# First v stage in a hand-computed list order, TensorE transposes for nine tiles, and other buffers and orders in an eight-core Trainium2 trunk kernel

## What is computed

```python
def trunk_layer(x, pool_buf, conv_buf, start_pos, pre_g, w_in, v_g, w_s, b_s,
                w_pg, pool_scale, conv_w, w_out, post_g):
    h = rmsnorm(x, pre_g)                                   # 1024 wide
    proj = jnp.einsum('bld,de->ble', h, w_in)
    u, v, z_a, p, z_b, xc, bg, cg, z_c = jnp.split(proj, IN_SPLITS, axis=-1)
    a_out, vn = chunk_gmlp(u, v, v_g, w_s, b_s)             # vn = rmsnorm(v, v_g), 768 wide
    b_out, new_pool = pool_mixer(p, pool_buf, start_pos, w_pg, pool_scale)
    c_out, new_conv = short_conv(xc, bg, cg, conv_buf, conv_w)
    mix = jnp.concatenate([a_out * jax.nn.silu(z_a), b_out * jax.nn.silu(z_b),
                           c_out * jax.nn.silu(z_c)], axis=-1)
    out = jnp.einsum('ble,ed->bld', mix, w_out)
    return x + rmsnorm(out, post_g), new_pool, new_conv, vn
```

## Time and profile before

| what | value |
| --- | --- |
| median of the runs shown | 2111.47 us |
| span of the profiled execution, slowest core (core 1) | 2096.3 us |
| spans of the eight cores | 2079.0 to 2096.3 us |
| TensorE busy | 2009.7 us, 96% of the span |
| VectorE, ScalarE, GpSimd busy | 52%, 27%, 17% |
| v stage of layer 0, first matmul to last | 25.75 to 82.8 us |
| bytes moved by DMA | 190.64 MB, mean 91 GB/s |

### The profile page before, as it was taken

How to read it: one execution, slowest core, us unless ns; L and a number is a source line. 1 busy time by engine, 2 the same in 40 slices (tenths; PEclk the granted TensorE clock), 3 DMA queues, 4 the chain that set the end, 5 groups by cost and what they waited for, 6 DMA issues and landing times.

```text
span 2096.3 us, 32513 instructions; the slowest of 8 cores (2079.0 to 2096.3 us)
## 1 busy us (share of the span) xinstructions
PE 2009.7 (96%) x10792; PEld 985.7 (47%) x10792; DVE 1086.2 (52%) x1592; ACT 574.4 (27%) x1117; POOL 366.2 (17%) x698
## 2 busy tenths in 40 slices
PE   4899999999989999999998999999999899999998
PEld 2445544444444544444454455444445345444443
DVE  3665555545455555554545555554554655555433
ACT  3431122222333122222332312222323221222211
POOL 4400010033320001103331001011333100110011
PEclk9999999999999999999999999999999999999999
DMA  9832333386333224418624323553861432234143
GB/s 233 159 55 39 66 62 60 61 180 182 96 70 58 37 61 81 79 35 200 193 52 75 63 31 67 70 81 65 205 174 35 80 66 40 43 61 70 68 153 131
DMA packets 141812, 190.64 MB, mean 91 GB/s; under 512 B 80976, under 2 KB 86736, under 8 KB 141648
## 3 DMA queue, kind: packets, MB, share of 16 engines
q0 software_dynamic: 41040, 71.39, 22.7%
q1 hardware_dynamic: 100608, 117.16, 19.5%
HBM read 199.70 MB, written 42.35 MB: 115 GB/s over the span
## 4 chain that ended last, share of the span: by engine, by line
PE 74%; DVE 7%; POOL 6%; DMA 5%; issue 5%; ACT 2%; SPq 1%; DVEq 0%; ACTq 0%; POOLq 0%
PE ps L389 59%; PE ps L672 7%; PE ps L435 6%; POOL sb_stats L382 5%; DVE sb_ar L368 3%; DVE sb_ar L364 3%; DMA sb_samp<-sp_in 2%; DMA sb_hT<-sb_hbuf 1%; POOL sb_stats L380 1%; ACT sb_hbuf L360 1%; DMA vs_o<-sb_ar 1%; PE ps L580 1%; PE ps L550 1%; ACT sb_ar L360 1%; SPq L373 0%
## 5 line engine op out<-in xcount | busy, mean ns | idle before, releaser
L389 PE MATMUL ps<-sb_hT,sb_ring 128*128 128x512 bf16 (+1 forms) x7040 | 1337.5, 349 | 0.3
L389 PEld LDWEIGHTS ps<-sb_hT,sb_ring 128*128 128x128 bf16 x7040 | 630.9, 98 | 653.7 <-issue 19.9
L360 ACT ACTIVATE sb_ar<-ps 128x512 f32<-128x512 f32 (+3 forms) x576 | 355.9, 622 | 852.3 <-PE ps L389 543.0
L672 PE MATMUL ps<-sb_wout,sb_mix 128*128 128x512 bf16 x2176 | 470.3, 379 | 3.0 <-issue 3.0
L672 PEld LDWEIGHTS ps<-sb_wout,sb_mix 128*128 128x128 bf16 x2176 | 212.6, 98 | 259.4 <-issue 3.6
L316 POOL DMA_DIRECT2D sb_ring<-w_t x176 | 94.8, 543 | 1018.5 <-PE ps L389 574.7
L435 PE MATMUL ps<-sb_ring,sb_hT 128*128 128x512 bf16 x1088 | 190.8, 340 | 46.6 <-DMA sb_hT<-sb_hbuf 33.1
L364 DVE TENSOR_TENSOR sb_ar<-ps,sb_ar 128x512 f32<-128x512 f32 (+1 forms) x240 | 145.7, 607 | 157.9 <-PE ps L389 155.8
L368 DVE SCALAR_TENSOR_TENSOR sb_ar<-sb_pcx,sb_convw,sb_ar 128x512 f32<-128x512 f32 x192 | 144.3, 752 | 92.8 <-ACT sb_ar L645 82.4
L368 DVE SCALAR_TENSOR_TENSOR sb_hbuf<-sb_ar,sb_stats,sb_pre_bc 128x1024 bf16<-128x1024 f32 x68 | 87.4, 1285 | 170.5 <-POOL sb_stats L382 158.1
L364 DVE TENSOR_TENSOR sb_pcx<-ps,sb_ar 128x512 f32<-128x512 f32 x96 | 66.5, 692 | 208.4 <-PE ps L389 208.4
(11 more groups left out here) (45 smaller groups left out, 489.8 us busy)
## 6 DMA issues: line engine op xcount, KB each, us to landing
sb_ring<-w_t POOLq DMA_DIRECT2D x176, 256.0 KB, 4.9
x_mid<-sb_ar SPq DMA_DIRECT2D x51, 512.0 KB, 3.0
...
```

Of the source, the lines that this page charges most:

```text
L360: return emit(ACT, lambda a: a.activation(out=out, in_=in_, func=func, scale=scale, **kw), reads=reads, writes=writes)
L389: ins = pe.matmul(bank(b, n), lhsT=wa.ap[:, k, :], rhs=hT[:, k, c0:c0 + n], start=(k == 0), stop=(k == 7))
L672: ins = pe.matmul(bank(b + half), lhsT=mix[:, k, j * 128:(j + 1) * 128], rhs=wout[:, k, half * 512:(half + 1) * 512], start=(k == 0), stop ...
```

## The change

- Layer 0's v stage is emitted in the order that a new function, `plan_first`, computes: a list scheduler with fixed durations and landing times, whose steps are sq, rs, nm (norm: square, rstd, scale), tp and ev (transpose on TensorE, copy out of PSUM) or dt (DMA transpose), mm (the 16 matmuls), vs, vr, vn (the same for v). Tiles 0 to 8 are transposed on TensorE, 8 transposes into one bank, and copied out by VectorE (even tiles) or ScalarE (odd ones); tiles 9 to 16 go by DMA as before.
- x tiles of layer 0 go into twelve buffers: four in `ar`, eight in the space of `wout`. Tiles 3 to 11 wait in SP's queue for pieces of w_v: tile 3 for piece 1, tile 4 for piece 3, tile 5 for piece 5, tiles 6 to 11 for piece 7.
- `pre_g` and `v_g` of layer 0 come as one row each (`rows0`, 7 KB together) and are spread over the partitions by four f32 matmuls with a row of ones, then copied by VectorE. A dummy activation is issued first on ScalarE.
- PSUM banks of layer 0's v stage are fixed: v tiles use three pairs (0 to 5) in turn, transposes banks 6 and 7.
- `sp_in` is loaded after the norm of tile 6 in layer 0, and in the out stage of the layer before (at tile 3) for layers 1 to 3.
- `b_stage` begins with slot 0 of the scratch ring.
- `c_stage` takes the chunks in the order 4, 0, 1, 2, 3.
- The last tile's norm of a layer follows the next layer's first v tile. There are 16 columns of statistics for 8.

Core of the diff, with the new functions:

```diff
@@ plan_first (new; the loop picks the ready step that can start first)
+    land_x = [5.0, 7.0, 9.0] + [12.5 + 2.2 * j for j in range(NT - 3)]
+    land_w = [9.5 + 1.4 * k for k in range(8)]
+    for j in range(NT):
+        steps["sq", j] = ("ACT", 1.25, [])
+        steps["rs", j] = ("POOL", 1.1, [("sq", j)])
+        steps["nm", j] = ("DVE", 1.28, [("rs", j)])
+        if j < N_PE_T:
+            steps["tp", j] = ("PE", 0.6, [("nm", j)])
+            steps["ev", j] = ("ACT" if j % 2 else "DVE", 1.15, [("tp", j)])
+            steps["mm", j] = ("PE", 2.6, [("ev", j)])
+        else:
+            steps["dt", j] = ("SP", 1.3, [("nm", j)])
+            steps["mm", j] = ("PE", 2.6, [("dt", j)])
+        steps["vs", j] = ("ACT", 1.0, [("mm", j)])
+        steps["vr", j] = ("POOL", 1.1, [("vs", j)])
+        steps["vn", j] = ("DVE", 1.02, [("vr", j)])
...
@@ helpers
+        def load_x0(j, after=()):
+            s = j % XSLOTS
...
+        def pe_transpose(j, b):
+            hb = j % NHB
+            pt = ps[:, 512 * b:512 * b + 512].bitcast(BF16)
+
+            def f(pe):
+                for k in range(8):
+                    ins = pe.transpose(pt[:, k * 128:(k + 1) * 128], hbuf[:, hb, k * 128:(k + 1) * 128], cstb[:, 0, :])
+                return ins
+            emit(PE, f, reads=[R_hb[hb], R["cstb"]], writes=[bank_res[b]])
+
+        def evac_transpose(j, b, q):
+            src = ps[:, 512 * b:512 * b + 512].bitcast(BF16).rearrange("p (k t) -> p k t", k=8)
+            dst = hT[:, :, j * 128:(j + 1) * 128]
...
@@ b_stage, c_stage
+            st["ar"] = 0
...
-                for ci, (c0, n) in enumerate(CHUNKS):
+                for ci in (4, 0, 1, 2, 3):
+                    c0, n = CHUNKS[ci]
...
@@ layer 0
+        emit(DVE, lambda v: v.memset(one, 1.0), writes=[r_one])
+        emit(SP, lambda s_: s_.dma_start(out=g_row, in_=rows0[:, 0:D]), writes=[r_row], dsem=d_row)
+        load_x0(0)
+        load_x0(1)
+        load_x0(2)
+        emit(SP, lambda s_: s_.dma_start(out=v_row, in_=rows0[:, D:D + WA]), writes=[r_vrow], dsem=d_vrow)
...
+        for j in range(3, XSLOTS):
+            load_x0(j, after=[wv0.kres[min(2 * j - 5, 7)].w])
...
+        spread(g_row, r_row, D, pre_bc[:], R["pre"], 0)
+        spread(v_row, r_vrow, WA, vb_bc[:], R["vb"], 2)
+        for kind, j in plan_first():
...
+            elif kind == "nm":
+                norm_h(j, stat_of[j])
+                if j + XSLOTS < NT:
+                    load_x0(j + XSLOTS)
+                if j == 6:
...
+                    sp_dma(samp[:], sp_in[0], [], [R["samp"]], d_c["samp"])
...
+                if j in (5, 7):
+                    ring_try()
+                elif j == 9:
+                    load_wpg(0)
+                elif j == 11:
+                    load_spatial(0)
@@ all layers
-                need(W[l]["v"])
-                for j in range(NT):
+                for j in range(1, NT):
                     v_job(l, j)
...
-            sp_dma(samp[:], sp_in[l], [], [R["samp"]], d_c["samp"])
...
+                if not last and j == 3:
+                    sp_dma(samp[:], sp_in[l + 1], [], [R["samp"]], d_c["samp"])
                 out_ew(l, j, b)
             if not last:
-                norm_h(NT - 1, norm_sq(NT - 1))
-                t_job(NT - 1)
+                need(W[l + 1]["v"])
+                v_job(l + 1, 0)
+                norm(NT - 1)
```

More of the change, by code:

```diff
@@ L62, in host_consts, with plan_first @@
     return cb.reshape(128, 256), np.ascontiguousarray(fac.reshape(128, 64))
+N_PE_T = 9
+XSLOTS = 12
+def plan_first():
+    land_x = [5.0, 7.0, 9.0] + [12.5 + 2.2 * j for j in range(NT - 3)]
+    land_w = [9.5 + 1.4 * k for k in range(8)]
+    free = {"PE": 0.0, "ACT": 0.0, "DVE": 0.0, "POOL": 0.0, "SP": 0.0}
+    done = {}
+    order = []
+    steps = {}
+    for j in range(NT):
[12 more added lines that the diff above has]
+        steps["vn", j] = ("DVE", 1.02, [("vr", j)])
+    lead = {"sq": 0.0, "rs": 0.0, "nm": 0.0, "tp": 0.2, "ev": 0.3, "dt": 0.3, "mm": 1.0,
+            "vs": 1.2, "vr": 1.2, "vn": 1.3}
+    nxt = {"mm": 0, "sq": 0}
+    left = dict(steps)
+    while left:
+        best = None
+        for (kind, j), (eng, dur, before) in left.items():
+            if any(d in left for d in before) or nxt.get(kind, j) != j:
+                continue
+            t = max([free[eng]] + [done[d] + 0.12 for d in before])
+            end = None
+            if kind == "sq":
+                t = max(t, land_x[j])
+                if j >= NHB:
+                    i = j - NHB
+                    gone = ("tp", i) if i < N_PE_T else ("dt", i)
+                    if gone in left:
+                        continue
+                    t = max(t, done[gone] + (0.0 if i < N_PE_T else 2.0))
+            elif kind == "tp" and j >= 2:
+                if ("ev", j - 2) in left:
+                    continue
+                t = max(t, done["ev", j - 2])
+            elif kind == "mm":
+                if j >= 3:
+                    if ("vn", j - 3) in left:
+                        continue
+                    t = max(t, done["vn", j - 3])
+                if j >= N_PE_T:
+                    t = max(t, done["dt", j] + 2.2)
+                end = t
+                for k in range(8):
+                    end = max(end, land_w[k]) + 0.325
+            key = (t, lead[kind] + j)
+            if best is None or key < best[0]:
+                best = (key, kind, j, eng, t, t + dur if end is None else end)
+        _, kind, j, eng, t, end = best
+        free[eng] = done[kind, j] = end
+        del left[kind, j]
+        if kind in nxt:
+            nxt[kind] += 1
+        order.append((kind, j))
+    return order
@@ L242, in build_nc @@
         R_ar = [Res() for _ in range(NAR)]
[L243 removed]
+        R_stat = [Res() for _ in range(NSTAT)]
         R_xd = [Res() for _ in range(NT)]
@@ L692, in out_ew @@
             sp_dma((y_o if l == DEPTH - 1 else x_mid)[j], x, rx, [R_xd[j]], d_xst[j])
-        AHEAD = 4
+        emit(POOL, lambda g: g.memset(neghalf[:], -0.5), writes=[R["neghalf"]])
+        emit(ACT, lambda a_: a_.activation(out=stats[:, 0:1], in_=neghalf[:], func=AF.Square),
+             reads=[R["neghalf"]], writes=[R_stat[0]])
+        g_row = mix[0:1, 0, :].bitcast(F32)[:, 0:D]
+        v_row = mix[0:1, 1, :].bitcast(F32)[:, 0:WA]
+        one = mix[0:1, 2, :].bitcast(F32)[:, 0:128]
+        r_row, r_vrow, r_one = Res(), Res(), Res()
@@ new lines, in spread @@
+        def spread(row, rr, n, dst, rd, b):
+            for h in range(0, n, 512):
+                m = min(512, n - h)
+                emit(PE, lambda pe: pe.matmul(bank(b + h // 512, m), lhsT=one, rhs=row[:, h:h + m], start=True,
+                                              stop=True), reads=[rr, r_one], writes=[bank_res[b + h // 512]])
+            emit(DVE, lambda v: v.tensor_copy(dst, ps[:, 512 * b:512 * b + n]),
+                 reads=[bank_res[b], bank_res[b + 1]], writes=[rd])
+        spread(g_row, r_row, D, pre_bc[:], R["pre"], 0)
```

108 lines of the change are left out of this document (67 added, 41 removed).

## The result

The changed kernel takes 2039.88 us in the median (2039.54 to 2040.35), against 2111.47 (2109.71 to 2113.31) for the kernel before beside it; the ratio is 0.9655, 95% interval 0.9638 to 0.9672. Runs in which the cores of one die had a lower clock than the rest are left out of every ratio and of all times. The forecast was 2049 with a range of 2036 to 2067: sign and size came out as forecast. That they did so this closely is in part luck: two errors in it were each as large as the difference of 9 us or larger, and of opposite signs: the first v stage was priced at 9.8 us and gave next to nothing in the profile, and the 15.2 us by which the median stood over the span, carried over from the kernel before, aren't there in the changed one.

A forecast was written before the change was run, and what follows sets the result against it. TensorE, busy 96% of the span, bounds the kernel; only its idle and low-clock time can be won. Gains of 38.6 + 11.1 + 3.0 + 9.8 = 62.5 us off 2096.3, plus 15.2, gave 2049 us, range 2036 to 2067.

The forecast's parts named there:

- Cores drawing together: Whole span: cores 1 and 6, at 2096.3 and 2079.0 us, differ by waits the change removes, so they converge.
- B stages: First group of each layer's B stage: waits for state and scratch slot go, VectorE is late next; gain 38.6 us.
- Starts of layers: Starts of layers 1 to 3: wait falls from 4.1 to 1.5 us, half the clock loss goes; gain 11.1 us.
- Rival B: B stages and layer starts: short waits left over each drop the clock, 5.1 + 3.3 us; 2057 us, chance 0.11.
- Chunk order: C stage: with the small chunk first, each layer's first out matmul no longer waits 0.74 us; gain 3.0 us.
- State load in the out stage: Out stages before layers 1 to 3: loading `samp` there costs nothing, or 0 to 3 us each if it collides.
- Rival D: Three out stages: the state load holds up SP's queue and x tiles come late; slower, 2121 us, chance 0.02.
- v stage of layer 0: Layer 0 before its B stage: the new order ends it at 73.0 us for 82.8; gain 9.8 us.
- 1.9 us of low clock: Beginning of layer 0's v stage: a term of 1.9 us for TensorE running at its lower clock.
- Copies out that TensorE waits for, 3.0: Layer 0's v stage: TensorE waits for three copies out of PSUM, 0.7 + 0.8 + 1.5 = 3.0 us.
- Rival A: Layer 0's v stage: transfers still set the pace, so it ends at 80 us; 2056 us, chance 0.13.
- 15.2 us added to the span: Whole kernel: the runs' median exceeds the profiled span by 15.2 us, added to 2033.8 to give 2049.0.

The follow-up runs named there:

- e12: e9 with four pairs of PSUM banks instead of three for v tiles from the tenth on; 2037.70 to 2040.16 us, ratio 0.9676 to the kernel before.
- e5: The changed kernel itself, no edit, measured again beside the kernel before; 2039.96 to 2040.65 us, ratio 0.9731.
- e1: The kernel before with every part of the change but layer 0's new v stage; 2043.5 to 2045.9 us, ratio 0.9763 to the kernel before.
- e3: The kernel before with only the early state loads; 2077.7 to 2079.6 us, ratio 0.9926 to the kernel before.
- e4: The kernel before with both scratch slot 0 at the B stage's start and the early state loads; 2061.1 to 2062.5 us, ratio 0.9844.
- e9: The changed kernel with only the planner's numbers replaced by those of its own trace; 2037.77 and 2037.80 us, ratio 0.9724 to the kernel before.
- e2: The kernel before with only the scratch ring set to slot 0 at the B stage's start; 2098.74 us, ratio 1.002.

## Why the prediction held, and where it didn't

*Cores drawing together.* Right: 2.4 us of spread for 17.3.

*B stages.* Right, and 2.7 us too low. The two waits went, and what was late next was VectorE, as said: waits of 0.43, 1.10, 0.91 and 0.89 us. The groups of layers 1 to 3 take 17.06, 16.87 and 16.85 where 16.9 was forecast. What was off is layer 0: 16.41 for 17.9, and without the half clock charged behind it (1.7). Its own terms held, on VectorE of the kernel after:

```profile
95.05 0.69 DVE L441 SCALAR_TENSOR_TENSOR sb_mix<-sb_pcx,sb_ar 128x512 bf16<-128x512 f32 x1
95.66 0.52 DVE L437 TENSOR_TENSOR sb_ar<-sb_samp 128x352 f32<-128x352 f32 x1
```

From the tree's start to the next group 3.49 us pass, for 3.57. But the fourth scale starts 12.31 us into the group, for 13.62 before: TensorE had stood 1.08 us ahead of the group for a bank, while VectorE went on. That is what made the wait smaller, and e12 bears it out from the other side: without the wait for the bank, VectorE is waited for 1.68 us.

*Starts of layers.* Right, 12.4 for 11.1. The wait is 1.90 for the 1.5 forecast, but the clock is kept behind it in all three layers, which I had taken by halves. Rival B, by which the short waits left over in B and at the starts would each drop the clock, is refuted here (waits of 0.9 to 1.9 us). It isn't by their length alone: in e5 a wait of 1.92 us in the v stage of layer 0, the third within 16 us, is followed by 9.64 us for 7.96.

*Chunk order.* Right, 3.0 in the profile; 5 us (3 to 7) in the timed runs.

*State load in the out stage.* Right: no gap in 110 us. Rival D fell here. In the v stage of layer 0 the same load isn't free: 1.5 to 2 us, as e1, e3 and e4 show.

*v stage of layer 0: this step failed.* The forecast was an end at 73.0, the B stage began at 82.74. Up to the end of the second v tile the sum came out: 23.3 + 2.6 + 1.9 = 27.8, and the row ends at 24.70 + 3.08 = 27.78. But that is chance: w_v came 1.4 us later than I had put, and the 1.9 us of low clock fell where TensorE had to wait for w_v anyway (3.33 us for 12 matmuls at 19.26, and then 3.08 for 18). Then 15 tiles and seven transposes, 42.5 us, were right too, transposes 0.45 us dearer. What failed are two terms, and one that was missing. "Copies out that TensorE waits for, 3.0" was 6.4 (2.68 + 1.22 + 2.52), and the waits for a bank pair, for which the sum had nothing, were 2.1 (1.02 + 1.08): together 8.5. I had costed each wait as transpose end to copy end, with the copy's own duration, too high even (1.15 for 0.68 on VectorE and 1.02 on ScalarE); but what TensorE waits for is the place of that copy in an in-order queue, behind a scaling that waits in turn for GpSimd, and, ahead of tile 13 and of the B stage, a scaling that holds one of three bank pairs. And the low clock, 1.9 us put ahead of all this, came again behind the two waits of 2.68 and 2.52: 9.64 for 7.96 and 14.84 for some 13.2, 3.3 us more (the granted clock reads 0.50 from 33 to 35 and from 57 to 59 us). The 10.86 for some 10.5 at 70.80 is not the clock, which reads 1.00 there, but small gaps, 0.3. 5.5 + 3.3 + 0.3 + 0.45 = 9.6, which is nearly the miss of 9.7. The prediction had named this: an order made for w_v at 19.3 us that holds VectorE at a step whose data is late. It stood under "what would make it wrong" and had no price.

That the order of the queues makes the waits is borne out by e9, where two of them shrank by 3.7 us with other numbers in the plan; e9 and e12 show why it brings at most 2 to 3: the wait for the bank pairs and, behind it, the last transpose and VectorE's B gates come next. Rival A named the right stage but not the cause: no v matmul waits for `sb_hT` from a DMA in the profile after.

*15.2 us added to the span.* Wrong as a step: it was taken for a constant of the measurement. The changed kernel's time is 1 us over its span (2040.35 and 2039.3). All later runs of the kernel before are 1 us over their slowest core's span too (2095.99 and 2094.9, the first beside e2), so the 15.2 us were no constant: the profiled execution was a faster one than the three that were timed. Without it the forecast would have been 2033.8, 6 us too low, the v stage's 9.7 less the 4 us that the B stages and the starts gave over their price. So the forecast was 9 us too high by one error of 15 one way and one of 6 the other.

Of the hardware, the rows above show one thing that bore on this: a power on GpSimd (L455) takes 0.57 us, beside a norm of VectorE from two SBUF tensors 1.43 (28.00 to 29.43, the norm ending at 29.00), and beside a scaling that reads PSUM 0.57 again (29.88). At 34.19 it takes 1.39 and again ends 0.43 us behind the norm beside it. The Trainium skill (SBUF — State Buffer, SBUF: two separate sides) says that VectorE with two SBUF inputs and a GpSimd operation that reads SBUF exclude each other on a shared port; the trace agrees, with 0.86 and 0.82 us.
